# Attention gates in a mixer layer: where the reciprocal is widened, where the gates stand in VectorE's queue, and when the first gate rows are requested

## What is computed

```python
h = rmsnorm(x, rms_g) * (1 + scale) + shift
q, k, v, z_a, glu, z_b, gates = jnp.split(h @ w_in + b_in, PROJ_SPLITS, axis=-1)
# 8 heads of 64; a latent token sees a window of 8 rows x 16 columns of latent keys, and all 256 context keys
p = jax.nn.softmax(jnp.concatenate([s_win, s_ctx], axis=-1), axis=-1).astype(v.dtype)
o = einsum('bhrckw,brkwhd->brchd', p_win, vb) + einsum('bhrcs,bshd->brchd', p_ctx, cv)
y_a = attend(q, k, v) * jax.nn.silu(z_a)
y_b = conv_branch(glu, dw_w, dw_b, ln_g, ln_b) * jax.nn.silu(z_b)
m = g_a * (y_a @ w_proj_a) + g_b * (y_b @ w_proj_b)
return x + gate * (m @ w_out), k, v
```

## Time and profile before

| | us |
|---|---|
| three runs | 1975.52, 1976.21, 1980.98; median 1976.21 |
| the profiled execution | 1978.27, its span 1976.5 |
| TensorE busy | 1870.8 (95%) |
| VectorE busy | 1068.9 (54%) |
| ScalarE busy | 527.5 (27%) |
| GpSimd busy | 123.4 (6%) |
| DMA | 235.08 MB, mean 119 GB/s |
| granted TensorE clock, mean | 0.989 of full speed |

### The profile page before, as it was taken

One profiled execution on the slowest core, in us unless ns is written; L12 is line 12 of the kernel. 1 busy time (PEld: TensorE's weight loads), 2 busy tenths in 40 slices (PEclk: granted clock), 3 DMA queues, 4 the chain that ended last, 5 costly groups with the idle time before them and its releaser, 6 DMA issues.

```text
span 1976.5 us, 27056 instructions
## 1 busy us (share of the span) xinstructions
PE 1870.8 (95%) x10707; PEld 1568.1 (79%) x10707; DVE 1068.9 (54%) x1713; ACT 527.5 (27%) x981; POOL 123.4 (6%) x221
## 2 busy tenths in 40 slices
PE   7999999999999999999999975888888899999998
PEld 1788899988888888888888865777777788878886
DVE  2544512121487088348708944777778755554443
ACT  2641101021111121111101123565656422221221
POOL 0000000000000000000000050121230000000000
PEclk9999999999999999999999997999999999999999
DMA  8525413232122022112201645777774466582421
GB/s 281 181 74 169 144 54 125 91 133 70 38 77 78 27 72 86 62 38 78 78 27 62 151 126 107 157 152 153 149 146 123 147 225 208 170 265 97 174 102 59
DMA packets 212041, 235.08 MB, mean 119 GB/s; under 512 B 47707, under 2 KB 158155, under 8 KB 208715
## 3 DMA queue, kind: packets, MB, share of 16 engines
q1 hardware_dynamic: 211656, 233.24, 40.3%
q10 hardware_dynamic: 259, 0.11, 0.0%
HBM read 152.52 MB, written 80.78 MB: 118 GB/s over the span
## 4 chain that ended last, share of the span: by engine, by line
PE 81%; DVE 8%; issue 5%; SPq 3%; DMA 2%; ACT 1%; DVEq 0%; POOL 0%; POOLq 0%; ACTq 0%
PE banks L759 16%; PE banks L761 16%; PE banks L760 16%; PE banks L1136 4%; PE banks L1634 3%; PE banks L1636 3%; PE banks L1635 3%; PE banks L1606 3%; PE banks L1607 3%; PE banks L1608 3%; DVE scores L1167 3%; PE banks L754 2%; PE banks L756 2%; PE banks L755 2%; DVE inv_wide L1191 1%
## 5 line engine op out<-in xcount | busy, mean ns | idle before, releaser
L759 PE MATMUL banks<-h_hi,w_hi 128*128 128x512 f32 (+1 forms) x1600 | 593.7, 371 | 2.5 <-DVE w_lo L544 1.5
L761 PE MATMUL banks<-h_hi,w_lo 128*128 128x512 f32 (+1 forms) x1600 | 589.9, 369 | 0.0
L760 PE MATMUL banks<-h_lo,w_hi 128*128 128x512 f32 (+1 forms) x1600 | 589.8, 369 | 0.0
L700 DVE SCALAR_TENSOR_TENSOR conv_acc<-glu_out,taps,conv_acc 128x773 f32<-128x773 f32 x360 | 371.9, 1033 | 12.3
L759 PEld LDWEIGHTS banks<-h_hi,w_hi 128*128 128x128 f32 x1600 | 302.0, 189 | 55.7 <-issue 2.6
L761 PEld LDWEIGHTS banks<-h_hi,w_lo 128*128 128x128 f32 x1600 | 301.8, 189 | 50.4
L760 PEld LDWEIGHTS banks<-h_lo,w_hi 128*128 128x128 f32 x1600 | 302.1, 189 | 48.9
L484 ACT ACTIVATE out_stage<-banks,param_cols 128x512 f32<-128x512 f32 (+1 forms) x120 | 77.0, 647 | 442.4 <-PE banks L761 436.7
L1242 ACT ACTIVATE probs<-scores,stat 128x640 f32<-128x640 f32 (+2 forms) x128 | 106.9, 835 | 130.3 <-DVE stat L1167 128.2
L1606 PE MATMUL banks<-y_hi,wp_hi 128*128 128x512 f32 (+1 forms) x320 | 120.8, 378 | 0.6 <-DVE y_lo L1779 0.5
L1608 PE MATMUL banks<-y_hi,wp_lo 128*128 128x512 f32 (+1 forms) x320 | 118.8, 371 | 0.0
(11 more groups left out here) (154 smaller groups left out, 2452.0 us busy)
## 6 DMA issues: line engine op xcount, KB each, us to landing
proj<-out_stage SPq DMA_DIRECT2D x96, 256.0 KB, 2.0
w_raw<-in_w_in SPq DMA_DIRECT2D x44, 512.0 KB, 4.0
gates_in<-proj SPq DMA_DIRECT2D x64, 256.0 KB, 3.1
k_hi<-k_hi_rows SPq DMA_DIRECT2D x16, 640.0 KB, 12.2
k_lo<-k_lo_rows SPq DMA_DIRECT2D x16, 640.0 KB, 14.2
w_ada<-in_w_ada SPq DMA_DIRECT2D x8, 1024.0 KB, 11.3
x_rows<-in_x_sample SPq DMA_DIRECT2D x4, 2048.0 KB, 11.4
x_out<-in_x_sample SPq DMA_DIRECT2D x16, 512.0 KB, 3.5
```

Of the source, the lines that this page charges most:

```text
L700: op = dve.scalar_tensor_tensor(dst, src, tap, dst, ALU.mult, ALU.add)
L759: pe.matmul(out, w_hi[:, s, k], h_hi[c][:, k], start=first, stop=False)
L760: pe.matmul(out, w_hi[:, s, k], h_lo[c][:, k], start=False, stop=False)
L761: op = pe.matmul(out, w_lo[:, s, k], h_hi[c][:, k], start=False, stop=last)
```

## The change

The reciprocal is taken of the two sums alone, into a new small buffer inv_sums; ScalarE then copies it 64-fold into inv_wide (`spread`), in its queue after the probability copy of the odd tile, and L1127's counterpart waits for that copy (wide_done). In VectorE's queue the gates of a pair stand ahead of the next tile's score row instead of behind it. And z of head 0 is requested inside the projection, as a fourth part, after chunk 3 of the last block, with a wait for the stores of the last block of z_a.

```diff
@@ -144,6 +144,8 @@
             lo_n += 1
         if kind in ("q", "k", "ck", "v"):
             qkv_out = list(per_slot)
+        if kind == "z" and blocks[n][1] < ZA0 + WA:
+            za_out = list(per_slot)
     full_of = {n: slot_of[u] for u, (kind, n, c) in enumerate(units) if kind == "k" and c == 4}
 
     done_after = {}
@@ -181,7 +183,7 @@
     gate_store_at = {spot(4, 1): 0, spot(5, 1): 1, spot(6, 1): 2, spot(9, 1): 3}
     gate_bias_at = {spot(4, 0): 0, spot(5, 0): 1, spot(6, 0): 2, spot(9, 0): 3}
     ck_load_at = spot(9, 1)
-    parts_at = {spot(nb - 1, c): c for c in range(3)}
+    parts_at = {spot(nb - 1, c): c for c in range(4)}
     io.gate = nc.dram_tensor("gate_rows_dram", (2, D), F32, kind="Internal").ap()
     io.q_hi, io.q_lo = (nc.dram_tensor(f"q_{h}_rows", (WA, TOK), F32, kind="Internal").ap() for h in ("hi", "lo"))
     io.k_hi, io.k_lo = (nc.dram_tensor(f"k_{h}_rows", (WA, KW), F32, kind="Internal").ap() for h in ("hi", "lo"))
@@ -398,6 +400,10 @@
             sp.wait_ge(low_d[s], low_per_slot[s])
         sp.wait_ge(tab_out, 16 * QC)
 
+    def za_stored(sp):
+        for s in range(3):
+            sp.wait_ge(out_d[s], za_out[s])
+
     def front_pool(pool):
         pool.memset(half[:], -0.5).then_inc(half_set, 1)
         pool.wait_ge(half_set, 1)
@@ -825,8 +831,9 @@
 
 
     io.front = (front_sync, front_pool, front_act, front_dve, front_pe)
+    io.za_stored = za_stored
     io.front_stored, io.qkv_stored, io.unit_mm, io.units_of_part = (
-        front_stored, qkv_stored, mm, [spot(nb - 1, c) + 1 for c in range(3)])
+        front_stored, qkv_stored, mm, [spot(nb - 1, c) + 1 for c in range(4)])
     io.ev_act, io.ev_dve, io.all_units, io.all_act, io.all_dve = ev_act, ev_dve, len(units), n_act, n_dve
 
 
@@ -901,7 +908,7 @@
     io.scores_at = used[0]
     s_sb, p_sb, pT = put("scores", [P, 2, 768]), put("probs", [P, 2, 768]), put("probs_t", [P, 4, 6, P])
     stat, sums = put("stat", [P, 4, 2]), put("exp_sums", [P, 4])
-    inv, z_inv = put("inv_wide", [P, 2, 2, DH]), put("z_scaled", [P, 2, P])
+    inv, inv_wide, z_inv = put("inv_sums", [P, 2, 2]), put("inv_wide", [P, 2, 2, DH]), put("z_scaled", [P, 2, P])
     z_sb, y_sb = put("z_halves", [P, 2, TOK // 2]), put("y_halves", [P, 2, TOK // 2])
     head_buffers(1)
     io.attn_end, io.room = 181280, nc.sbuf_top - io.mem
@@ -916,7 +923,7 @@
     s_mm, red, exp_done = sem("scores_mm"), sem("minima"), sem("exp_done")
     tr_done, pt_dve, pt_act, pv_done, z_scaled = (sem("probs_turned"), sem("pt_dve"), sem("pt_act"), sem("pv_done"),
                                                   sem("z_scaled"))
-    inv_done, y_done, y_out = sem("inv_done"), sem("y_done"), [sem("y_out0"), sem("y_out1")]
+    inv_done, wide_done, y_done, y_out = sem("inv_done"), sem("inv_spread"), sem("y_done"), [sem("y_out0"), sem("y_out1")]
 
     PAIRS = [(8 * e + b, 8 * e + 4 + b) for e in range(2) for b in range(4)] + [(LT, LT + 1)]
     PPH = len(PAIRS)
@@ -1023,6 +1030,9 @@
             if part == 1:
                 load_window(q, 0)
                 load_v(0)
+            if part == 3:
+                io.za_stored(q)
+                load_z(0)
             if part == 2:
                 q.dma_start(rmask[:], io.row_mask.rearrange("t p r -> p t r")).then_inc(mask_in, 16)
                 q.dma_start(cmask[:], io.col_mask.rearrange("t p r -> p t r")).then_inc(mask_in, 16)
@@ -1042,7 +1052,6 @@
         load_window(sp, 1)
         load_qk(1)
         load_v(1)
-        load_z(0)
         load_z(1)
         tail_stage.load_first(sp)
         for n in range(2, HEADS):
@@ -1121,10 +1130,10 @@
             n = BODY[m][0]
             if m % TPH == 0:
                 pe.wait_ge(v_in[n % 2], 288 * (n // 2 + 1))
-            pe.wait_ge(inv_done, k + 1)
+            pe.wait_ge(wide_done, k + 1)
             if k:
                 pe.wait_ge(y_done, k)
-            pe.transpose(ps_inv, inv[:, k % 2].rearrange("p e d -> p (e d)"), cst.ident[:])
+            pe.transpose(ps_inv, inv_wide[:, k % 2].rearrange("p e d -> p (e d)"), cst.ident[:])
             pe.wait_ge(pt_act, m + 2)
             pe.wait_ge(pt_dve, m + 2)
             both = [values_of(m), values_of(m + 1)]
@@ -1186,9 +1195,9 @@
 
             dve.wait_ge(exp_done, 2 * k + 2)
             if k >= 2:
-                dve.wait_ge(pv_done, 2 * (k - 1))
+                dve.wait_ge(wide_done, k - 1)
             at = 2 * k % 4
-            dve.reciprocal(inv[:, k % 2], sums[:, at:at + 2].unsqueeze(2).to_broadcast([P, 2, DH])).then_inc(inv_done, 1)
+            dve.reciprocal(inv[:, k % 2], sums[:, at:at + 2]).then_inc(inv_done, 1)
 
         def gate_out(k):
 
@@ -1219,10 +1228,10 @@
                 copy_window(m)
                 if m % 2:
                     invert(m // 2)
+            if m >= 3 and m % 2:
+                gate_out(m // 2 - 1)
             if m + 2 < NT:
                 soften(m + 2)
-            if m >= 3 and m % 2:
-                gate_out(m // 2 - 1)
             tail_stage.early_dve(dve, m)
         tail_stage.dve(dve)
 
@@ -1251,12 +1260,21 @@
             first = 0 if nb else 1
             act.activation(pT[:, m % 4, 3 + first:6], ps_t[1][:, first:3], ACT.Copy).then_inc(pt_act, 1)
 
+        def spread(k):
+
+            act.wait_ge(inv_done, k + 1)
+            if k >= 2:
+                act.wait_ge(pv_done, 2 * (k - 1))
+            act.activation(inv_wide[:, k % 2], inv[:, k % 2].unsqueeze(2).to_broadcast([P, 2, DH]), ACT.Copy).then_inc(wide_done, 1)
+
         exponents(0)
         for m in range(NT + 1):
             if m + 1 < NT:
                 exponents(m + 1)
             if m < NT:
                 copy_rest(m)
+                if m % 2:
+                    spread(m // 2)
             tail_stage.early_act(act, m)
         tail_stage.act(act)
```

## The result

| | us |
|---|---|
| before, four runs | 1975.52 to 1980.98, median 1976.78 |
| after, four runs | 1917.22 to 1921.72, median 1918.77 |
| ratio | 0.9705, 95% interval 0.9686 to 0.9723 |
| the profiled execution of after | 1918.94, its span 1917.1 |
| predicted | 1913, range 1902 to 1930 |

The change gives 58 us. The forecast is 5.8 us too low. The interval is 3.7 us wide to either side, so something is left to explain besides the gain.

A forecast was written before the change was run, and what follows sets the result against it. No engine is full; a loop of waits bounds attention, plus one stall for z. Gains of 32.2 (first head), 32 (six heads) and 2.5 (last), less 3 for GpSimd, sum to 63.7: 1913 us, range 1902 to 1930.

The forecast's parts named there:

- The reciprocal on VectorE: Attention pair loop: the two-element reciprocal holds VectorE's queue 0.1 us, ends 0.05 and 0.2, freeing 0.76 us a pair.
- ScalarE's copy: Attention pair loop: ScalarE's widening copy takes 0.25 us, other end 0.37, hidden between the probability copy and the next exponential.
- The gates ahead: VectorE's queue: gate done 1.6 us after the odd turn, 1.1 before TensorE needs it; the wait on y_halves goes.
- The pair: Steady heads: 4.42 us for each of six pairs plus 11.6 for three beside the context, 38.1 a head against 43.4.
- What limits the pair: TensorE in the pair loop: the even tile's turn waits behind ScalarE's copy of the odd one, 1.44 to 1.54 us.
- z: Start of attention: requesting z inside the projection removes the stall; the first two pairs gain 29.0 us at zero cost.
- the slow pair: First head: the 7.1 us pair after the stall, slowed by TensorE's clock, returns 2.7 us with the stall.
- The last head: Head with eight weight conversions: 4.75 us a pair, 2.5 us gained in all, ends 0 and 5.
- The wait for GpSimd: Layer norm step in heads 2 and 4: VectorE waits 2.0 us behind the table, twice; 3 us given back.
- each round now waits for its start: SP's load queue: argument against rival B, since SP stands idle from 1267.8 to 1275.6 before the next round.
- Rival B, the loads: Attention loads set the head: tables take 38 to 41 us, heads 40 to 41, time 1926; chance 0.12.

The follow-up runs named there:

- small steps ahead: The changed kernel with GpSimd's two small layer norm steps put ahead of the bias tables of heads 3 and 5; 1906.86 us, ratio 0.9638.
- z alone: The kernel before with only head 0's z requested inside the projection, old reciprocal and gate order kept; 1951.96 us, ratio 0.9862.
- without z: The changed kernel with head 0's first z requested after the projection as before; 1941.88 us, ratio 0.9811.
- the tail's requests moved: The changed kernel with the tail's three first requests in head 3's round of loads, not ahead of head 2's; 1913.1 us, ratio 0.9667.

## Why the prediction was right, and where it was off

The time lies in the forecast's own range, and by the mechanism that it named. Point by point:

- **The reciprocal on VectorE.** Forecast 0.1 us of the queue, measured 0.08 (1184.98 to 1185.06). The operation itself is 0.154 long in place of 0.943, and the next began before its end. Right.
- **ScalarE's copy.** Forecast 0.25, other end 0.37, measured 0.306 and hidden. The figure from the Trainium skill, "VectorE: DVE Perf Modes", section on the TRN2 errata, gave an estimate of 0.29, which is nearer than my line through the larger copies. Nothing hung on it: three more of them cost 2.5 us in all.
- **The gates ahead.** Forecast at +1.6, measured at +1.78 and 1.1 us ahead of TensorE (+2.91). The wait before L1127 is gone but for one of 1.3 us. Right.
- **The pair.** Forecast 4.42 us for the six wide pairs and 11.6 for the three beside the context, measured 4.35 (4.29 to 4.00) and 11.73. A head 38.1 against 37.8. Right. With GpSimd's wait out of the way the six heads gain 34.2 us (263.57 - 229.39, small steps ahead) against 32 forecast.
- **What limits the pair.** The forecast named the even turn's wait for ScalarE's copy. Turn to turn is 1.53 as it said (1.44 to 1.54), but the products moved between the turns took nothing off. That experiment only moves the wait, so it neither confirms nor refutes the claim. It stays open; that TensorE is busy 38.40 of 40 us says there is little left in it.
- **z.** Forecast 29.0 for the first two pairs, measured 29.25. The clock in 1165 to 1202 is 0.95, so the slow pair went with the stall. The forecast's 2.7 us for it held a part of the pair's own shortening; by z alone it was 2.0. Head 0 gave 3.82 behind the stall where 3.2 was forecast, because seven pairs follow there and the forecast counted six; its 0.53 a pair is near the measured 0.55. The requests take 3.65 us of SP's time at 1157.88 and every eviction near them waits for TensorE alone, none for a slot. Right.
- **The last head.** Forecast 2.5 with ends 0 and 5, measured 5.13: its pairs take 4.40, where I took 4.75 (by which eight pairs give 2.3, not 2.5). Mis-sized, without a reason from a row for the 4.75.
- **The wait for GpSimd, the step that failed.** Forecast 2.0 us twice, 3 given back. Measured waits of 8.4 and 3.3 and, by the experiment with the small steps ahead, 11.6 us given back. The size came from two times counted from the start of a round: VectorE at L1755 after 32.4, the table after 33.4, plus 1. Measured in the round of head 5, which started on time at 1326.19: VectorE at 1357.91, 31.7 after, the table at 1360.20, 34.0 after. Those are off by 0.7 and 0.6 and make the 3.3. In the round of head 3 another 5.0 us come on top, since it started that late; with that round on time, without z, the wait was 3.9. The prediction had checked that "each round now waits for its start", for the kernel before, and took over from it that every round starts with the scores. But taking the stall away moved the round of head 2 by 28 us, up against z of head 1 and the tail's three requests, which had before been issued during the stall. SP had no idle time there any more.
- **The first turn 1.45 us later.** Not forecast. The projection's last eviction came at 1164.55 before and the first turn 7.55 later; in after at 1165.32 and 8.23 later; with the small steps ahead, which has the same requests, at 1164.95 and 7.54 later. Over the nine profiled kernels with the requests and this order on TensorE the first turn lies anywhere from 1170.33 to 1174.21, and in the two without them at 1172.10 and 1172.09. So it is chance of a profiled run, and no cost of the requests is shown.
- **Rival B, the loads.** Not the case that came, but its mechanism did in one round: that of head 2 took 40.6 us (1204.47 to 1245.06) where a head takes 37.8. The later rounds took no longer than the work.

The sum in measured terms: 29.25 + 3.82 + 34.2 - 11.6 + 5.13 - 1.45 = 59.3. The wait was forecast 8.6 us too cheap, and everything else together 4.2 us too low (34.2 for 32, 5.13 for 2.5, 0.9 at head 0, less the 1.45): two errors of opposite sign, the larger one in a single term. That the small ones offset half of it is luck.

## What to carry to other kernels

When a stall is removed, list what used to happen during it. Here SP issued the next head's z and the tail's first loads under cover of the stall, and without the stall these and the slower issue behind them put the next two rounds 2.2 and 5.0 us behind their start. In a queue that works in order, put the short step that an engine waits for ahead of the long one that nobody needs yet: two operations of 0.8 us together behind a table of 9.7 us were worth 12 us of the kernel's time, a fifth of what the whole change brought. And of two edits at one loop, measure each alone and read a steady head beside the time: the reciprocal and the order took 3.5 and 2.5 us off a head and 5.7 together, but 25 and 18 us off the time and 32 together, because the wait for GpSimd grew elsewhere.

## What the runs showed of the hardware

A stop of TensorE of 7.37 us is followed by work at the lower clock: 0.50 in 1280 to 1284, 0.78 in 1284 to 1288, 1.00 from there on. The pair that holds the stop took 13.67 us where it takes 4.19 in the kernel with the small steps ahead, 9.5 more for a wait of 8.4. How much of it is the clock and how much the refilling of the loop is not separated.

SP's time for the sixteen v_win requests of head 2 was 18.61 us before the change, 20.16 with the tail's requests moved and 23.14 in the changed kernel; in the changed kernel's later rounds it was 17.13 to 19.30. The issue of a load is no constant, and a sum over SP's queue made from an unhurried round comes out too small.
